# Half of the first modulation tiles unsplit, x and modulation loads interleaved, the other eight groups summed on the vector engine

## What is computed

```
mod = silu(c) @ w_ada + b_ada             # c: 2 rows (prompt, sample); w_ada: 1024 x 6144
sh1, sc1, g1, sh2, sc2, g2 = split(mod, 6)
h   = rmsnorm(x, g_norm1) * (1 + sc1) + sh1
z   = h @ w_in                            # 1024 x 2464
... attention, retention and stick-breaking heads on z, output projection; x = x + g1 * mix
... h = rmsnorm(x, g_norm2) * (1 + sc2) + sh2; gated MLP with a short convolution; x = x + g2 * f
y   = rmsnorm(x, g_final)
```

## Time and profile before

| | us |
|---|---|
| median of 3 runs | 1782.06 (1781.98 to 1783.7) |
| profiled execution | 1783.8 |
| its span, first to last instruction | 1782.1 |
| PE busy in the span | 1671.7 (94%) |
| DVE busy | 1060.8 (60%) |
| ACT busy | 645.0 (36%) |
| first matmul of the first z tile | 62.8 |
| end of the last z tile | 348.3 |
| mean granted TensorE clock | 0.966 of full speed |

### The profile page before, as it was taken

How to read it: one execution, slowest core, us unless ns; L and a number is a source line. 1 busy time by engine, 2 the same in 40 slices (tenths; PEclk the granted TensorE clock), 3 DMA queues, 4 the chain that set the end, 5 groups by cost and what they waited for, 6 DMA issues and landing times.

```text
span 1782.1 us, 27943 instructions
## 1 busy us (share of the span) xinstructions
PE 1671.7 (94%) x10051; PEld 1498.6 (84%) x10051; DVE 1060.8 (60%) x2269; ACT 645.0 (36%) x1252; POOL 179.6 (10%) x235
## 2 busy tenths in 40 slices
PE   6699999989788999999998999999999999999996
PEld 3499999835556677777898999999999999999996
DVE  5843333237687766767525666666666666666657
ACT  7522211225555656667424422221222122212213
POOL 0011111122333212311120000000000000000000
PEclk9899999978889999999999999999999999999999
DMA  9264444431121101005410111111111111111003
GB/s 347 81 233 153 137 129 141 136 108 37 40 92 47 43 16 47 4 13 173 148 48 13 48 48 60 36 47 35 59 35 47 35 59 35 47 35 59 12 1 113
DMA packets 114423, 133.63 MB, mean 75 GB/s; under 512 B 15003, under 2 KB 91722, under 8 KB 113002
## 3 DMA queue, kind: packets, MB, share of 16 engines
q1 hardware_dynamic: 110953, 121.83, 21.2%
q0 software_dynamic: 3328, 10.73, 1.7%
q10 hardware_dynamic: 64, 0.07, 0.0%
HBM read 107.54 MB, written 27.29 MB: 76 GB/s over the span
## 4 chain that ended last, share of the span: by engine, by line
PE 85%; DVE 7%; ACT 4%; issue 3%; DMA 1%; SPq 0%; DVEq 0%; ACTq 0%; POOLq 0%
PE psum L2002 33%; PE psum L2066 15%; PE psum L1783 13%; PE psum L1971 5%; PE psum L1924 3%; PE psum L1868 2%; PE psum L1953 2%; PE psum L1928 2%; PE psum L1822 1%; PE psum L1817 1%; PE psum L1718 1%; PE psum L1849 1%; PE psum L1719 1%; DVE h_lo L1356 1%; DVE act_lo L1356 1%
## 5 line engine op out<-in xcount | busy, mean ns | idle before, releaser
L2002 PE MATMUL psum<-act_hi,wt_parts 128*128 128x362 f32 (+1 forms) x2496 | 615.6, 328 | 9.5 <-DVE act_lo L1356 5.2
L1655 DVE SCALAR_TENSOR_TENSOR residual<-psum,mod,residual 128x364 f32<-128x364 f32 (+2 forms) x704 | 299.8, 496 | 257.6 <-PE psum L2066 257.6
L2002 PEld LDWEIGHTS psum<-act_hi,wt_parts 128*128 128x128 f32 x2496 | 442.3, 189 | 12.2 <-issue 6.8
L2002 PE MATMUL psum<-act_lo,wt_parts 128*128 128x362 f32 (+1 forms) x1248 | 409.0, 328 | 0.0
L2066 PE MATMUL psum<-u_hi,wt_parts 128*128 128x362 f32 (+1 forms) x1056 | 263.3, 331 | 3.0 <-issue 3.0
L2002 PEld LDWEIGHTS psum<-act_lo,wt_parts 128*128 128x128 f32 x1248 | 235.6, 189 | 0.0
L2066 PEld LDWEIGHTS psum<-u_hi,wt_parts 128*128 128x128 f32 x1056 | 188.1, 189 | 3.3 <-issue 3.3
L1783 PE MATMUL psum<-w_hi,h_hi 128*128 128x308 f32 (+1 forms) x576 | 177.6, 308 | 12.1 <-DVE h_lo L1356 10.9
L1783 PE MATMUL psum<-w_lo,h_hi 128*128 128x308 f32 (+1 forms) x576 | 177.0, 307 | 0.0
L1783 PE MATMUL psum<-w_hi,h_lo 128*128 128x308 f32 (+1 forms) x576 | 176.5, 306 | 0.0
L2066 PE MATMUL psum<-u_lo,wt_parts 128*128 128x364 f32 (+1 forms) x528 | 174.7, 331 | 0.0
(11 more groups left out here) (222 smaller groups left out, 2289.3 us busy)
## 6 DMA issues: line engine op xcount, KB each, us to landing
wt_raw<-in_w_up SPq DMA_DIRECT2D x44, 512.0 KB, 3.8
ada_raw<-in_w_ada SPq DMA_DIRECT2D x32, 512.0 KB, 4.1
wt_raw<-in_w_down SPq DMA_DIRECT2D x22, 512.0 KB, 4.3
w_raw<-in_w_in SPq DMA_DIRECT2D x16, 616.0 KB, 6.9
z_scratch<-z_out POOLq DMA_DIRECT2D x64, 154.0 KB, 2.3
z_in<-z_scratch SPq DMA_DIRECT2D x8, 1232.0 KB, 5.3
ada_first<-in_w_ada SPq DMA_DIRECT2D x16, 512.0 KB, 11.5
xT_scratch<-xT SPq DMA_DIRECT2D x1, 4352.0 KB, 15.6
```

The source lines that it names most:

```text
L1655: last = dve.scalar_tensor_tensor(out=res[:, d, a:b], in0=bank[4 + q % 4][:, a - CHUNKS[c][0]:b - CHUNKS[c][0]], scalar=mod[:, 40 + d, whi ...
L2002: last = pe.matmul(out[:, :b - a], ww[:, slot, P * k:P * k + P], aa[:, k, a:b], start=(k == 0 and m == 0), stop=(k == KT - 1 and m == 2))
```

## The change

The first four modulation groups keep their place on PE, but of the two tiles of a piece the first is multiplied unsplit, as plain float32 with `c_whole` (silu(c) in two columns and two columns of zeros); only the second is split. PE's order becomes: x tiles 0 to 2, vectors, spread, group 0, tiles 3 to 5, spread, group 1, tiles 6 to 8, spread, group 2, group 3. SP loads x0, the vectors, x1 and x2, group 0, x3 to x5, group 1, x6 to x8, group 2, w_in, group 3, and the second w_in group as soon as its buffers are free.

The other eight groups leave PE's row form. DVE multiplies each 128x512 tile with a per-partition scalar of silu(c), once for each of the two rows of c, and adds up over the eight k in `ada_acc`: a piece is four DVE instructions. `ADA_AT` places the 32 pieces in the z groups 1 to 7, `ADA_SUMS` the places where PE sums a finished group over the partitions: eight fp32 matmuls with a 128x128 block of `ada_acc` as weights and one column of ones, which yield mod in columns, in bank 5. The store to DRAM, the load back and PE's transpose go.

The normalisation has five runs, cut at tile borders (128, 384, 640, 896), and is done in one go on DVE. In the first z group PE waits for h step by step, ACT copies the z tiles and then splits the second w_in group between the copies 4 and 5. The loops over z groups are written out on PE, ACT, DVE and SP.

```diff
-NORM_RUNS = ([(0, 128), (128, 364), (364, 726), (726, 1088)], CHUNKS)
+NORM_RUNS = ([(0, 128), (128, 384), (384, 640), (640, 896), (896, 1088)], CHUNKS)
+ADA_AT = {1: 5, 2: 5, 3: 5, 4: 5, 5: 4, 6: 4, 7: 4}
+ADA_SUMS = {(2, 1): 0, (3, 1): 1, (4, 1): 2, (5, 1): 3, (5, 3): 4, (6, 1): 5, (7, 1): 6, (7, 8): 7}
+def ada_pieces(g, t):
+    at = (-1, 1, 3, 5, 7)[:ADA_AT.get(g, 0)]
+    return [sum(ADA_AT.get(x, 0) for x in range(g)) + at.index(t)] if t in at else []
...
 # SP
+            load_x(0)
             ... the nine vectors
+            load_x(1)
+            load_x(2)
             for g in range(ADA_A - 1):
                 load_first(g)
+                if g < 2:
+                    for t in range(3 * g + 3, 3 * g + 6):
+                        load_x(t)
             load_w_in(0, 0)
             load_w_in(0, 1)
             load_first(ADA_A - 1)
-            load_ada(ADA_A)
+            for half in range(2):
+                sp.wait_ge(s_wlo, half + 1)
+                load_w_in(1, half)
+            for p in range(4):
+                load_ada(p)
...
 # ACT
+            def ada_high(g):
+                for i in range(4):
+                    act.wait_ge(s_first[4 * g + i], 16)
+                    if g:
+                        act.wait_ge(s_adamm, 4 * (g - 1) + i + 1)
+                    act.activation(ada_hi[:, i], ada_first[:, g, i, 1], ACT.Copy).then_inc(s_ahi, 1)
+            ada_high(0)
             x_chunk(1)
+            ada_high(1)
+            copy_row(0)
             x_chunk(2)
             copy_rstd(2)
+            ada_high(2)
+            copy_row(1)
+            split_w_in(0, 0)
+            ada_high(3)
+            copy_row(2)
+            copy_row(3)
...
+            h_high(0, 0)
+            h_high(0, 1)
+            copy_z(0)
+            h_high(0, 2)
+            copy_z(1)
+            copy_z(2)
+            h_high(0, 3)
+            copy_z(3)
+            copy_z(4)
+            h_high(0, 4)
+            split_w_in(1, 1)
+            for t in range(5, NTILE):
+                copy_z(t)
...
 # DVE
+            def ada_sum(p):
+                g, q = divmod(p, 4)
+                dve.wait_ge(s_ada[q], 16 * (g + 1))
+                if q == 0 and g >= 2:
+                    dve.wait_ge(s_asum, g - 1)
+                for k in (2 * q, 2 * q + 1):
+                    for c in range(2):
+                        total, w = ada_acc[:, g % 2, c], ada_raw[:, q, k % 2]
+                        if k == 0:
+                            ins = dve.tensor_scalar(total, w, silu_c[:, c, k:k + 1], None, ALU.mult)
+                        else:
+                            dve.wait_ge(s_acc, 16 * g + 2 * (k - 1) + c + 1)
+                            ins = dve.scalar_tensor_tensor(out=total, in0=w, scalar=silu_c[:, c, k:k + 1], in1=total,
+                                                           op0=ALU.mult, op1=ALU.add)
+                        ins.then_inc(s_acc, 1)
...
+            norm(0, range(len(NORM_RUNS[0])))
+            split_w_in(1, 1, 0)
+            split_w_in(1, 1, 1)
+            for g in range(1, NZG):
+                z_group(g)
...
 # PE
+            def ada_first_group(g):
+                if g >= 2:
+                    pe.wait_ge(s_row, g - 1)
+                out = bank[4 + g % 2][0:4, :]
+                for i in range(4):
+                    pe.wait_ge(s_first[4 * g + i], 16)
+                    pe.matmul(out, c_whole[:, 2 * i, :], ada_first[:, g, i, 0], start=(i == 0), stop=False)
+                    pe.wait_ge(s_alo, 4 * g + i + 1)
+                    pe.matmul(out, c_parts[:, 2 * i + 1, :], ada_hi[:, i, :], start=False, stop=False)
+                    last = pe.matmul(out, c_parts[:, 2 * i + 1, :], ada_lo[:, i, :], start=False, stop=(i == 3))
+                    last.then_inc(s_adamm, 1)
+            def ada_columns(g):
+                pe.wait_ge(s_acc, 16 * (g + 1))
+                if g == 0:
+                    pe.wait_ge(s_row, ADA_A)
+                for j in range(AG // P):
+                    for c in range(2):
+                        at = 2 * (AG // P * g + j) + c
+                        last = pe.matmul(bank[5][:, at:at + 1], ada_acc[:, g % 2, c, P * j:P * j + P], ones[:, 0:1],
+                                         start=True, stop=True)
+                last.then_inc(s_asum, 1)
...
                     for k in range(KT):
+                        if g == 0:
+                            pe.wait_ge(s_h, 8 * chunk_of(t, NORM_RUNS[0]) + k + 1)
...
                     last.then_inc(s_z, 1)
-                    if t % 2:
-                        ada_piece(g + ADA_A, t // 2)
+                    if (g, t) in ADA_SUMS:
+                        ada_columns(ADA_SUMS[g, t])
...
-            pe.wait_ge(s_modl, 16)
-            pe.transpose(bank[7][:, 0:P], mod_rows[:], ident[:]).then_inc(s_modt, 1)
```

More of the change, by code:

```diff
@@ L552, in load_first, with load_ada @@
                         .then_inc(s_first[4 * g + q], 16)
[L554 to L559, removed]
+            def load_ada(p):
+                if p >= 4:
+                    sp.wait_ge(s_acc, 4 * (p - 3))
+                g, q = ADA_A + p // 4, p % 4
+                sp.dma_start(ada_raw[:, q], w_ada_v[:, 2 * q:2 * q + 2, AG * g:AG * g + AG]).then_inc(s_ada[q], 16)
             def load_w_in(g, half):
@@ L962, in _ @@
-            copy_row_a(ADA_A - 1)
-            for c in range(len(NORM_RUNS[0])):
-                h_high(0, c)
-                if c == 0:
-                    ada_high(ADA_A, 0)
-                    ada_high(ADA_A, 1)
-            def group(g, slot, first=False, last=False):
-                if not first:
-                    store_row(g - 1, 1 - slot)
-                    act.wait_ge(s_z, 9 * g)
-                    ada_high(g + ADA_A, 0)
-                if not last:
-                    split_w_in(g + 1, 1 - slot)
-                for q in range(2 if first else 1, 4):
-                    ada_high(g + ADA_A, q)
@@ L980, in _, with copy_z @@
-            group(0, 0, first=True)
-            group(1, 1)
-            with act.Fori(1, 3) as i:
-                for s in range(2):
-                    group(2 * i + s, s)
-            group(NZG - 2, 0)
-            group(NZG - 1, 1, last=True)
-            store_row(NZG - 1, 1)
+            ada_high(2)
+            copy_row(1)
+            act.wait_ge(s_xt, 2 * NTILE)
+            split_w_in(0, 0)
+            ada_high(3)
+            copy_row(2)
+            copy_row(3)
+            def copy_z(t):
+                act.wait_ge(s_z, t + 1)
+                if t >= 3:
+                    act.wait_ge(s_zst[t % 3], 16 * (t // 3))
+                act.activation(z_out[:ROWS[t], t % 3, :], bank[t % 3][:ROWS[t], 0:ZG], ACT.Copy).then_inc(s_zc0, 1)
@@ L1338, in normed @@
                 if k == 0:
-                    dve.wait_ge(s_rb, 3 * n + next(i for i, x in enumerate(CHUNKS) if NORM_RUNS[n][c][1] <= x[1]) + 1)
+                    dve.wait_ge(s_rb, 3 * n + next(i for i, x in enumerate(CHUNKS if n else X_RUNS) if NORM_RUNS[n][c][1] <= x[1]) + 1)
                 if j >= 3:
@@ L1377, in z_group @@
                     dve.tensor_copy(z_out[:ROWS[t], t % 3, :], bank[t % 3][:ROWS[t], 0:ZG]).then_inc(s_zc, 1)
[L1378 to L1385 removed]
+                    for p in ada_pieces(g, t):
+                        ada_sum(p)
```

269 lines of the change are left out of this document (109 added, 160 removed).

## The result

The changed kernel takes 1761.38 us (median of four runs, 1760.34 to 1764.97) against 1782.66 of the kernel before on the same chip: ratio 0.9884, 95% interval 0.9867 to 0.9901, that is 21.3 us less. The forecast was 1763 us with a range of 1752 to 1773. The profiled execution took 1761.96 us, its span is 1760.3.

What follows compares the result with a forecast made beforehand. PE was taken to bound projection groups 1 to 7. First stage 64.5, group 0 39.5 and later groups 225.4 end the projection at 329.4 against 348.3 (-18.9); with tail -0.2, 1763 us, range 1752 to 1773.

Steps and rivals of the forecast that it cites:

- 1. Later groups: Input projection groups 1 to 7: PE sheds modulation pieces, gains 1.7 us column blocks; 225.4 us instead of 240.0.
- rival C: Later projection groups stay at 34.2 us each, z paced by copies or stores rather than PE; 1777 us, chance 0.05.
- Rival D: Later groups: one-column blocks do not hide weight loads, 5.5 us a block, 27 more in all; 1790 us, chance 0.05.
- 2. First stage: Start to normalisation: PE's strict order puts x transposes behind modulation groups; ends at 64.5 us, 7.0 later than before.
- N: Start of normalisation on DVE, the end of the first stage; forecast at 64.5 us, bounds 60 and 84.
- The bound without the lower clock: First stage: normalisation starts at 60 us if no quarter of a modulation group runs at PE's lower clock.
- Rival A: First stage no later than before, normalisation at about 58 (x1 sooner or PE's clock never drops); 1757 us, chance 0.15.
- Rival B: PE at its lower clock all first stage, normalisation at 84; 1782 us, chance 0.11 including the stretch down to the forecast.
- 3. Group 0: First z group, from normalisation's start: 39.5 us against 50.9, so 11.4 gained; tile 8 waits for ACT's copy.
- 4. Tail: Behind the projection: path through the last store and DVE unchanged, except one addition less, 0.2 us gained.

Runs made afterwards that it cites:

- e1: Changed kernel with the eight matmuls that turn a group's sums into columns run twice in each of eight groups; 1782.66 us, ratio 0.9994 to the kernel before.
- e9: Changed kernel with PE's waits ahead of the second and third spread and z group 0 filled with useless identity transposes; 1758.22 us.
- e8: Changed kernel in its interleaved first-stage order, but with all eight k tiles of the first modulation groups split; 1760.31 us.
- e11: Kernel before with the later eight modulation groups' sums on DVE, two row banks and PE's step-by-step waits for h in group 0; 1762.18 us.
- e3: Changed kernel with all nine x tiles loaded first and done in threes ahead of all but half of modulation group 0, half unsplit; 1761.49 us.
- e2: Changed kernel with ACT copying z tile 5 of group 0 ahead of the high halves of the next w_in; 1761.74 us.
- e10: Changed kernel with the earlier kernel's first-stage order, a quarter of k tiles unsplit, two row banks, z tile 5 copied first and PE's waits filled; 1750.53 us.
- e4: Changed kernel with all nine x tiles first in threes, and all k tiles of the first modulation groups split; 1761.32 us.
- e7: Changed kernel with the earlier kernel's four normalisation runs and DVE copying group 0's z tiles, the last run behind tile 1; 1772.0 us.

## Why the prediction was right

**1. Later groups, forecast -14.6, measured -13.5.** Right in mechanism and price. The block of columns, which no row of before showed, was put at 1.7 and is 1.68; the product at 0.75 and is 0.743. The 1.1 us are the tiles: nine in 30.66, not 30.5. DVE's group is 17.7 us on average (124 / 7); the 20.4 forecast was for a group with five pieces, and with 32 pieces in seven groups its terms give 18.9. So rival C had no ground. Rival D (unhidden weight loads) is out by the 0.105 us a record. e1 has a near relation that the prediction missed: a block twice as long is slower through the clock.

**2. First stage, forecast N = 64.5, measured 65.74.** The pieces came near what was worked out: second spread 31.63 (33.1 forecast), third 47.51 (48.8). From there to the end of group 3 it took 16.4 us where 13.8 were forecast: a quarter is 1.51 at the upper level, not 1.36, and the second one behind the spread is slow too. The earlier spread paid half of that. The bound without the lower clock was 60; e9 measured 60.92. Rival A (N near 58) fell with it. Rival B's worst end (84) did not come: the clock is back at 1.00 a few us behind each wait. One sentence was too simple: it named the x transposes behind the groups as the price. The interleaved order that puts them there is a sufficient cause (10.3 us, e8 against e11; the lower level behind the longer waits is part of it), but putting x first in threes brought 0.6 us with half unsplit (e3): there PE is busy for all of 38 to 58 us with the groups.

**3. Group 0, forecast -11.4, measured -13.2.** The wait ahead of tile 8 for ACT's copy is there, 1.22 us in the changed kernel, and taking the copy forward is worth 1.4 (e2):

```profile
99.97 0.35 PE L1810 MATMUL psum<-w_hi,h_hi 128*64 128x308 f32 x1 [1.22 <-ACT z_out L965]
```

Tile 8 starts at N + 34.2, not 36.1. What was too dear is ACT's copies: 2.1 us of DVE waiting for ACT were charged, 0.6 is seen between N and 98 us.

**4. Tail, forecast -0.2, measured -3.4.** The mechanism was missed. The removed addition is 0.22 us, but without it the next instruction of DVE starts just ahead of a product of POOL instead of 0.14 us behind it, and so does a later one. The kernel before:

```profile
359.98 1.27 POOL L780 TENSOR_TENSOR rope_a<-z_in,rope_t 64x512 f32<-64x512 f32 x1 [0.18 <-POOL kr L783]
...
360.12 1.16 DVE L1330 SCALAR_TENSOR_TENSOR scale_n<-mod,vec_a 128x16 f32<-128x16 f32 x1
...
363.06 1.11 DVE L1441 TENSOR_SCALAR zqn<-z_in,rs 64x384 f32<-64x384 f32 x1
```

The changed kernel:

```profile
341.39 0.17 DVE L1340 SCALAR_TENSOR_TENSOR scale_n<-mod,vec_a 128x16 f32<-128x16 f32 x1
341.51 1.27 POOL L797 TENSOR_TENSOR rope_a<-z_in,rope_t 64x512 f32<-64x512 f32 x1 [0.18 <-POOL kr L800]
...
343.35 0.41 DVE L1446 TENSOR_SCALAR zqn<-z_in,rs 64x384 f32<-64x384 f32 x1
```

e10 has it as the kernel before:

```profile
326.90 1.40 POOL L800 TENSOR_TENSOR rope_a<-z_in,rope_t 64x512 f32<-64x512 f32 x1 [0.18 <-POOL kr L803]
327.31 1.02 DVE L1346 SCALAR_TENSOR_TENSOR scale_n<-mod,vec_a 128x16 f32<-128x16 f32 x1
```

The two instructions cost 1.5 to 1.7 us more when POOL is first. e10 lacks the addition too, so its removal does not decide the order alone: there one of POOL's products ahead (`rope_b`) takes 0.21 us, against 0.59 to 0.63 in the others, and POOL comes first all the same. POOL is first in the kernel before and in e10, which need 1433.8 and 1434.2 us behind the z stage, and in none of the other twelve profiles, which need 1429.2 to 1431.7. Each of these is a single execution. The rest of the 3.4 us lies later and was not followed; that it comes from the same collision is only argued.

The forecast total was off by 1.6 us; its four terms by 1.1, 1.2, 1.8 and 3.2, two of either sign. That the total came so close is luck: with the tail as forecast, and all else as measured, the time would have been 3.2 us longer.

## What to carry to other kernels

Where one engine is busy for all of a stretch, moving work off it paid one for one here, and the new form's price can be taken from the nearest row of the same shape. Ahead of such a stretch, where engines hand work round, the order of one engine's list decides: keep a tile ready for each engine before another stands at a wait, and test order and cost apart, because here they did not add. A gain of a few us in front can be lost or won again further on by which of two engines comes first to a shared resource.

## What the runs showed of the hardware

- **One-column fp32 matmuls and the clock.** Eight of them (sixteen records, 1.68 us) between z tiles leave the clock at 1.00; sixteen in a row (3.46 us) were followed by z matmuls at the lower level (0.26 us apart against 0.14) behind six of seven such blocks in the profiled execution of e1; the heap of times that it belongs to holds half of the executions.
- **The clock behind a wait.** In the first stages of the kernel before, the changed kernel, e3, e4, e8 and e11 the stretches at the lower level follow waits of PE of 2.0 to 4.1 us; filled with useless transposes, the same instructions run at the upper level (e9). A wait of that length is not always followed by one: behind 2.44 us (second spread, kernel before and e11) and 2.89 us (e7, group 0) the clock stayed at 1.00. The Trainium skill (TensorE: Matmul & The Clock Gate, "HAM oscillation — how this bites in real kernels") tells of bursts that start throttled after each wait; e9 agrees for the changed kernel's waits, at 4.8 us for this stage.
- **DVE and POOL.** A 16-column product of DVE with two inputs in SBUF takes 0.17 us alone and 1.02 to 1.16 when a product of POOL of 1.27 to 1.40 us has begun first. The Trainium skill (SBUF — State Buffer, "Who interferes with whom") says that such an instruction and a GpSimd one that reads SBUF exclude each other, and that the one that issues first holds the ports to its end. The rows agree.
